# Hymba-style decoder step: a store and a state piece issued behind the next up loads on SyncE's queue

## Chip, core and metric

The kernel runs on one core of a Trainium2 chip. The metric is the device time of one execution in microseconds, lower is better. TensorE does the matmuls, VectorE (DVE), ScalarE (ACT) and GpSimd (POOL) the elementwise work, and SyncE (SP) issues most DMAs. All DMAs of the core share 16 DMA engines.

## What is computed

One step of a decoder layer on 1032 tokens (1024 prompt, 8 samples) of width 1024: a mixer (an mLSTM head group and an HGRN2 head group), then a mixture of 16 gated-MLP experts, of which each token takes two, each part with a residual and a layer norm. The change touches the second part only:

```python
def _hmoe(x, w_rg, b_rg, w_re, b_re, w1, w3, w2):
    ...
    eid = g[:, None] * EXPERTS_PER_GROUP + top_i
    gate = jnp.einsum('nk,nke->ne', wts, jax.nn.one_hot(eid, N_EXPERTS, dtype=F32))
    a = jnp.einsum('nd,edf->nef', xt, w1)
    u = jnp.einsum('nd,edf->nef', xt, w3)
    hdn = jax.nn.silu(a) * u * gate[..., None].astype(x.dtype)
    return jnp.einsum('nef,efd->nd', hdn, w2).reshape(B, T, D)
```

Each expert has a gate and an up matrix (1024x256) and a down matrix (256x1024), 1 MB each in f32. The step also returns new states of the 8 samples (`out_C_s`, `out_S_s`).

## The kernel before

The first 770 us are projections and the chunked mixer. Then come the router and the expert stage, from 805 us to 1086 us of the span, in 20 expert steps (`STEPS`), numbered 0 to 19 here. In a step 128 rows (tokens sorted by expert) are worked on, 32 for each of four streams (`STREAMS`). A stream walks through its experts in order, so a weight matrix is loaded only when the stream's next step has another expert; a load has a condition register (`cond=new`) and moves nothing otherwise. In a run of the expert stage 15 experts are loaded so, beside the four that were there at the start. Each stream has one buffer for each of the gate, up and down matrices, so a matrix can be loaded only once the products with the old one are over.

TensorE's order in step n: gate products of n (L1387), transposition of the hidden rows of n-1 (L1373), transposition of the x rows of n+1 (L1347), down products of n-1 (L1362), up products of n (L1398). Undisturbed a step takes about 11.8 us.

SyncE runs a queue in written order. In step n it waits for `gate_done` of n and issues the gate loads of n+1 (L1251); it waits for `down_done` of n-1 and issues the down loads of n (L1257); then `store_y(n - 1)` (L1284) waits until VectorE has added the down products of n-1 to the scaled residual (`y_read`) and stores 128 rows (512 KB) to `y_slots` in DRAM; in odd steps 3 to 17 `store_states` (`out_dma`, L474) stores one eighth of the samples' states, 512 KB; then SyncE waits for `up_done` of n and issues the up loads of n+1 (L1254). Ahead of the gate loads, and again ahead of the down loads, it reads the expert numbers and flags from SBUF (L1263, TENSOR_LOAD). In even steps up to 14 a load of `v_piece` (512 KB, L1272) follows the gate loads, and the 1 MB of layer-norm parameters for the end (L1311) are issued once, between steps 11 and 12.

The rows of x (512 KB for each step) are gathered by GpSimd on a queue of its own, q0. `ysb` has four buffers: ScalarE fills that of step n for n+4 once its store has landed. GpSimd gathers the stored rows only after the last store.

Of the kernel before, what the change touches and what calls it, by code (L numbers as in the profile page):

```python
# [31 lines left out]
H = 4  # L32
# [81 lines left out]
def _program(nc, t, ctx):  # L114
# [358 lines left out]
    def out_dma(eng, dst, src):  # L473
        eng.dma_start(dst, src).then_inc(s.outputs, 16)  # L474
        outs[0] += 1
# [41 lines left out]
    def x_rows(c):  # L517
        return P if c < NCH else NS
# [7 lines left out]
    def sync_rest(sp):  # L526
# [29 lines left out]
        for n, c in enumerate(ROW_ORDER):  # L556
# [26 lines left out]
            sp.dma_start(x1_dram[c * P:c * P + r], xrow_of(c)[0:r]).then_inc(s.x1_written, 16)  # L583
        sp.wait_ge(s.x1_written, 16 * NTT)
        sync_moe(sp)

    def samples_product(pe, bank, groups):
# [643 lines left out]
    def is_first(pair, i=0):  # L1231

        return isinstance(pair, int) and pair == 0 and i == 0
# [11 lines left out]
    def sync_moe(sp):  # L1245
        wg = t["w_gate"].rearrange("e (p k) f -> e p k f", k=KD)
        wu = t["w_up"].rearrange("e (p k) f -> e p k f", k=KD)
        wd = t["w_down"].rearrange("e (p k) n -> e p k n", k=2)

        def load_gate(q, expert, new):  # L1250
            sp.dma_start(w_gate[q], wg[bass.ds(expert, 1)].rearrange("e p k f -> p (e k) f"), cond=new).then_inc(s.w_gate_in, 16)  # L1251

        def load_up(q, expert, new):
            sp.dma_start(w_up[q], wu[bass.ds(expert, 1)].rearrange("e p k f -> p (e k) f"), cond=new).then_inc(s.w_up_in, 16)  # L1254

        def load_down(q, expert, new):
            sp.dma_start(w_down[q], wd[bass.ds(expert, 1)].rearrange("e p k n -> p (e k) n"), cond=new).then_inc(s.w_down_in, 16)  # L1257

        def experts_of(n):

            def words(w, top):
                row = step_loads[0:1, bass.ds((n * 2 + w) * STREAMS, STREAMS)]
                return nc.values_load_multi_w_load_instructions(row, engines=[mybir.EngineType.SP], min_val=0, max_val=top,  # L1263
                                                                skip_runtime_bounds_check_because="experts are minima with NE - 1, flags come from a comparison")[1]

            experts, flags = words(0, NE - 1), words(1, 1)
            return [(q, experts[q], flags[q]) for q in range(STREAMS)]

        def load_v(piece):
            if piece >= 1:  # L1270
                sp.wait_ge(s.state_added, 2 * piece)
            sp.dma_start(v_piece, v_dram[piece:piece + 1].rearrange("a (b v) -> a b v", b=NS).partition_broadcast(P).rearrange("p a b v -> p (a b) v")).then_inc(s.v_piece_in, 16)  # L1272

        sp.wait_ge(s.experts_known, 1)
        early_outs.append(outs[0])

        def store_states(piece):
            kind, at = piece // H, 8 * piece % HB
            sp.wait_ge(s.state_added, 2 * piece + 2)
            out_dma(sp, (t["out_C_s"], t["out_S_s"])[kind].rearrange("p h b v -> p (h b) v")[:, at:at + 8], (C0, S0)[kind][:, at:at + 8])  # L1280

        def store_y(n):
            sp.wait_ge(s.y_read, 2 * n + 2)
            sp.dma_start(y_slots[n * P:(n + 1) * P], ysb[n % YBUFS]).then_inc(y_out[n % YBUFS], 16)  # L1284

        def step(pair, i, last):
            n = pair * 2 + i
            if not (last and i == 1):
                coming = experts_of(n + 1)
                sp.wait_ge(s.gate_done, pair * 2 + (i + 1))  # L1290
                for q, expert, new in coming:
                    load_gate(q, expert, new)
                if i == 0 and pair < 2 * H:
                    load_v(pair)
            if not is_first(pair, i):
                present = experts_of(n)
                sp.wait_ge(s.down_done, n)
                for q, expert, new in present:
                    load_down(q, expert, new)
                store_y(n - 1)  # L1300
                if i == 1 and 1 <= pair <= 2 * H:
                    store_states(pair - 1)
            if not (last and i == 1):
                sp.wait_ge(s.up_done, pair * 2 + (i + 1))
                for q, expert, new in coming:
                    load_up(q, expert, new)

        def between(pair):

            if pair == 6:  # L1310
                sp.dma_start(ln2_gb, t["ln2"].partition_broadcast(P)).then_inc(s.ln2_in, 16)  # L1311

        for pair in range(STEPS // 2):
            between(pair)
            for i in range(2):
                step(pair, i, pair == STEPS // 2 - 1)
        store_y(STEPS - 1)
        early_outs.append(outs[0])
        for n, c in enumerate(ROW_ORDER):
            r = x_rows(c)  # L1320
            if n < Y_SHIFTED:
                sp.wait_ge(s.y_ready, n + 1)
            else:
                sp.wait_ge(s.y_last, NCH + n - Y_SHIFTED)
            out_dma(sp, t["out_y"][c * P:c * P + r], pair_of[c][0:r, 0])
        sp.wait_ge(s.outputs, 16 * outs[0])
# [823 lines left out]
```

## Time and profile before

| | us |
|---|---|
| median of three runs | 1131.74 |
| lowest and highest run | 1127.57, 1140.96 |
| profiled execution, its own time | 1135.78 |
| its span from first to last instruction | 1133.9 |
| TensorE busy | 1052.6 |
| SyncE's DMA queue q1 | 125.96 MB |

The trace is of one execution, and its span is 1.9 us under that execution's time. TensorE is busy for 93% of the span, with a mean granted clock of 0.972 of full speed. Where it stands still in the expert stage, the chain of waits names what it stood for.

### The profile page before, as it was taken

What the parts mean: (1) busy time and instruction counts of PE and PEld (TensorE: products, weight loads), DVE (VectorE), ACT (ScalarE), POOL (GpSimd) and SP (SyncE); (2) the same over time, 40 slices, a digit from 0 to 9 for tenths busy, and PEclk for the clock granted to TensorE, in tenths of its full rate; (3) what the DMA queues carried; (4) which work ended last, traced back from release to release, by engine and by line L of the source; (5) the groups of instructions that cost most, each with busy time, mean ns of one, the idle gap of its engine ahead of it and who ended that gap; (6) DMA issues with size and microseconds to landing.
All of it is one profiled execution on the core that took longest, in us unless ns stands there. A gap on an engine that the chain in (4) does not pass through costs nothing.

```text
span 1133.9 us, 17432 instructions
## 1 busy us (share of the span) xinstructions
PE 1052.6 (93%) x6876; PEld 621.2 (55%) x6876; DVE 543.7 (48%) x987; ACT 273.8 (24%) x557; POOL 211.2 (19%) x202
## 2 busy tenths in 40 slices
PE   7999999979999988899999999999889899899856
PEld 4666666645656545565665666655444554455322
DVE  1541033354564547668666765837334333332137
ACT  1552111121222223323332333311111111111113
POOL 0000000000110113245435534500100000000056
PEclk9999999989999989899999999999999999899978
DMA  9120202020000054201011001059599986957756
GB/s 380 62 75 1 75 1 74 1 78 0 2 0 1 1 182 174 89 20 38 1 38 38 20 19 38 19 204 373 210 380 344 350 298 190 368 205 234 249 207 259
DMA packets 30476, 150.10 MB, mean 132 GB/s; under 512 B 5603, under 2 KB 6051, under 8 KB 21323
## 3 DMA queue, kind: packets, MB, share of 16 engines
q1 hardware_dynamic: 24730, 125.96, 30.0%
q0 software_dynamic: 5248, 18.94, 4.7%
q10 hardware_dynamic: 432, 4.35, 1.0%
q8 instruction: 38, 0.62, 0.2%
q14 instruction: 28, 0.22, 0.1%
HBM read 317.31 MB, written 23.82 MB: 301 GB/s over the span
## 4 chain that ended last, share of the span: by engine, by line
PE 83%; DMA 8%; DVE 5%; issue 2%; SPq 1%; ACT 0%; POOL 0%; DVEq 0%; POOLq 0%; ACTq 0%
PE psum L1725 18%; PE psum L784 10%; PE psum L1776 10%; PE psum L797 8%; PE psum L1398 5%; PE psum L1362 5%; PE psum L825 4%; DMA x_cm<-in_w_up 4%; PE psum L1387 4%; PE psum L1410 2%; PE psum L1743 1%; DMA hg_q<-in_w_down 1%; PE psum L759 1%; PE psum L1347 1%; DMA weight_slots<-in_w_gate 1%
## 5 line engine op out<-in xcount | busy, mean ns | idle before, releaser
L1725 PE MATMUL psum<-x_cm,weight_slots 128*128 128x344 f32 x720 | 209.0, 453 | 0.0
L1725 PEld LDWEIGHTS psum<-x_cm,weight_slots 128*128 128x128 f32 x720 | 136.6, 190 | 71.9 <-issue 1.1
L1776 PE MATMUL psum<-weight_slots,x_cm 128*128 128x512 f32 x256 | 113.6, 597 | 0.0
L1362 PE MATMUL psum<-conv_qk,scratch 128*32 128x512 f32 x320 | 75.9, 618 | 7.9 <-DMA hg_q<-in_w_down 3.5
L1398 PE MATMUL psum<-conv_qk,scratch 128*32 128x256 f32 x640 | 74.4, 386 | 9.1 <-DMA x_cm<-in_w_up 9.1
L1387 PE MATMUL psum<-weight_slots,scratch 128*32 128x256 f32 x1280 | 75.6, 389 | 6.5 <-DMA weight_slots<-in_w_gate 4.2
L1776 PEld LDWEIGHTS psum<-weight_slots,x_cm 128*128 128x128 f32 x256 | 47.9, 192 | 54.2 <-issue 54.2
L1362 PE MATMUL psum<-hg_q,scratch 128*32 128x512 f32 x320 | 75.9, 619 | 0.0
L1398 PE MATMUL psum<-hg_decay,scratch 128*32 128x256 f32 x320 | 74.2, 386 | 0.0
L1398 PE MATMUL psum<-x_cm,scratch 128*32 128x256 f32 x320 | 74.2, 386 | 0.0
L825 PEld LDWEIGHTS psum<-scratch 128*128 128x128 f32 x448 | 58.7, 193 | 24.4 <-issue 22.7
L1479 POOL DMA_INDIRECT scratch<-x_rows,hg_k x20 | 19.0, 948 | 276.4 <-ACT scratch L1434 110.6
L1041 POOL TENSOR_TENSOR scratch<-scratch,hg_k 128x256 f32<-128x256 f32 x56 | 45.5, 812 | 104.5 <-ACT scratch L940 104.3
L1398 PEld LDWEIGHTS psum<-conv_qk,scratch 128*32 128x32 f32 x640 | 38.3, 111 | 46.3 <-DMA x_cm<-in_w_up 14.8
L1387 PEld LDWEIGHTS psum<-weight_slots,scratch 128*32 128x32 f32 x1280 | 43.8, 113 | 35.8 <-issue 6.1
L825 PE MATMUL psum<-scratch 128*128 128x128 f32 x448 | 59.8, 277 | 2.0 <-POOL scratch L1041 2.0
L2002 DVE TENSOR_SCALAR scratch<-scratch,small 128x1024 f32<-128x1024 f32 x8 | 6.5, 813 | 114.9 <-ACT scratch L1861 114.9
L1129 DVE COPY_PREDICATED scratch<-level_masks,psum 128x512 f32<-128x512 uint8 x64 | 46.9, 734 | 25.7 <-PE psum L827 22.5
L784 PE MATMUL psum<-weight_slots,x_cm 128*128 128x512 f32 x128 | 58.2, 597 | 0.0
L940 ACT ACTIVATE scratch<-scratch 128x512 f32<-128x512 f32 x56 | 35.3, 630 | 93.9 <-DVE scratch L1124 93.8
L1944 POOL TENSOR_TENSOR scratch<-scratch,constants 128x512 f32<-128x512 f32 x8 | 10.2, 1272 | 256.5 <-ACT scratch L1917 256.5
L784 PE MATMUL psum<-conv_qk,x_cm 128*128 128x512 f32 x128 | 57.8, 594 | 0.0
(390 smaller groups left out, 1678.8 us busy)
## 6 DMA issues: line engine op xcount, KB each, us to landing
weight_slots<-in_w_gate SPq DMA_DIRECT2D x80, 1024.0 KB
conv_qk<-in_w_up SPq DMA_DIRECT2D x40, 1024.0 KB
conv_qk<-in_w_down SPq DMA_DIRECT2D x40, 1024.0 KB
hg_q<-in_w_down SPq DMA_DIRECT2D x40, 1024.0 KB
hg_decay<-in_w_up SPq DMA_DIRECT2D x20, 1024.0 KB
x_cm<-in_w_up SPq DMA_DIRECT2D x20, 1024.0 KB
weight_slots<-in_w_in SPq DMA_DIRECT2D x6, 2048.0 KB, 8.2
y_slots<-scratch SPq DMA_DIRECT2D x10, 512.0 KB, 7.9
```

Of the source, the lines that this page charges most:

```text
L784: i = mm(PS[:, bank, :], xT[:, k, c * P:(c + 1) * P], w_slot(g)[:, k, :], start=(k == 0), stop=(k == KD - 1))
L797: i = mm(PS[:, 6 + n, :], lhs, w_out[:, e, n * 512:(n + 1) * 512], start=(e == 0), stop=(e == 7))
L825: i = mm(hp(2 + n % 2, h), xl[:, h], xl[:, h], start=True, stop=True)
L940: tell(A(xlev[n % 2], xlev[n % 2], ACT.Exp), s.level_exp)
L1041: tell(g.tensor_tensor(x, x, y, ALU.mult), s.level_scaled)
L1129: tell(v.copy_predicated(amat, msk[:, l:l + 1, :].to_broadcast([P, H, P]), by_h(PS[:, 2 + n % 2, :])), s.level_kept)
L1362: m = mm(PS[lane, 5 + half, :], hidT[:, k, lane], w_down[q][:, k, half * 512:(half + 1) * 512], start=(k == 0), stop=(k == 1))
L1387: m = mm(PS[lane, 2, 0:FF], xgT[i][:, k, lane], w_gate[q][:, k], start=(k == 0), stop=(k == KD - 1))
L1398: m = mm(PS[lane, 3, 0:FF], xgT[i][:, k, lane], w_up[q][:, k], start=(k == 0), stop=(k == KD - 1))
L1410: m = mm(PS[:, 2 * (n % 4) + half, :], ident, pair_of[c][:, k, half * 512:(half + 1) * 512], start=(k == 0), stop=(k == 1))
L1725: i = mm(PS[0:m, idx % 4, 0:PIECE], lhs_of(k), xT[:, k, n * PIECE:(n + 1) * PIECE], start=(k == 0), stop=(k == KD - 1))
L1776: i = mm(PS[:, bank, :], xT[:, k, c * P:(c + 1) * P], w_slot(g)[:, k, :], start=(k == 0), stop=(k == KD - 1))
```

## The change

The two stores move as a block from behind the down loads to behind the up loads. Nothing else differs: the same DMAs of the same size and the same waits. In step 19, which has no up loads, and after it the order is as before.

```diff
                 for q, expert, new in present:
                     load_down(q, expert, new)
-                store_y(n - 1)
-                if i == 1 and 1 <= pair <= 2 * H:
-                    store_states(pair - 1)
             if not (last and i == 1):
                 sp.wait_ge(s.up_done, pair * 2 + (i + 1))
                 for q, expert, new in coming:
                     load_up(q, expert, new)
+            if not is_first(pair, i):
+                store_y(n - 1)
+                if i == 1 and 1 <= pair <= 2 * H:
+                    store_states(pair - 1)
```

The helpers that it calls are these:

```python
def store_states(piece):
    kind, at = piece // H, 8 * piece % HB
    sp.wait_ge(s.state_added, 2 * piece + 2)
    out_dma(sp, (t["out_C_s"], t["out_S_s"])[kind].rearrange("p h b v -> p (h b) v")[:, at:at + 8], (C0, S0)[kind][:, at:at + 8])

def store_y(n):
    sp.wait_ge(s.y_read, 2 * n + 2)
    sp.dma_start(y_slots[n * P:(n + 1) * P], ysb[n % YBUFS]).then_inc(y_out[n % YBUFS], 16)
```

SyncE's queue at the seam of steps 11 and 12, before. The down loads write `conv_qk` and `hg_q`, the up loads `conv_qk`, `hg_decay` and `x_cm`, the gate loads `weight_slots`:

```order
L1257 DMA hg_q<-in_w_down 128x2048
L1284 DMA y_slots<-x_cm 128x1024
L474 DMA out_S_s<-weight_slots 128x1024
L1254 DMA conv_qk<-in_w_up 128x2048 x2
L1254 DMA hg_decay<-in_w_up 128x2048
L1254 DMA x_cm<-in_w_up 128x2048
L1311 DMA hg_k<-in_ln 128x2048
L1263 TENSOR_LOAD hg_k x2
L1251 ISA
L1251 DMA weight_slots<-in_w_gate 128x2048
```

The same place with the change (lines behind the diff count one higher):

```order
L1257 DMA hg_q<-in_w_down 128x2048
L1254 DMA conv_qk<-in_w_up 128x2048 x2
L1254 DMA hg_decay<-in_w_up 128x2048
L1254 DMA x_cm<-in_w_up 128x2048
L1284 DMA y_slots<-x_cm 128x1024
L474 DMA out_S_s<-weight_slots 128x1024
L1312 DMA hg_k<-in_ln 128x2048
L1263 TENSOR_LOAD hg_k x2
L1251 ISA
L1251 DMA weight_slots<-in_w_gate 128x2048
```

Both stores have moved past the four up loads and stand directly ahead of what follows in the next step. In an even step the block is the store of rows alone. The difference at such a place, the store of step 1's products in step 2:

```order
-L1284 DMA y_slots<-scratch 128x1024
-L1254 DMA conv_qk<-in_w_up 128x2048 x2
-L1254 DMA hg_decay<-in_w_up 128x2048
-L1254 DMA x_cm<-in_w_up 128x2048
-L1263 TENSOR_LOAD hg_k x2
```

The store of rows stood ahead of the up loads there; with the change it stands between them and the two TENSOR_LOADs.

## Rows read from the trace of the kernel before

**Rows 1.** The page, chain that ended last: share of the span by engine

```profile
PE 83%; DMA 8%; DVE 5%; issue 2%; SPq 1%; ACT 0%; POOL 0%; DVEq 0%; POOLq 0%; ACTq 0%
```

**Rows 2.** TensorE's waits from 805 to 1095 us: total, times, longest

```profile
PE psum L1398 <- DMA x_cm<-in_w_up: 9.1, 5, 3.4
PE psum L1387 <- DMA weight_slots<-in_w_gate: 4.2, 2, 3.7
PE psum L1362 <- DMA hg_q<-in_w_down: 3.5, 2, 2.5
PE psum L1362 <- issue: 2.7, 2, 2.1
```

**Rows 3.** Timeline of SyncE's queue in step 5: start, length, instruction

```profile
886.21 0.34 SPq L1284 DMA_DIRECT2D y_slots<-scratch  x1
886.60 1.31 SPq L474 DMA_DIRECT2D out_C_s<-x_cm  x1
888.24 0.54 SPq L1254 DMA_DIRECT2D conv_qk<-in_w_up  x2
...
891.92 1.14 SPq L1251 DMA_DIRECT2D weight_slots<-in_w_gate  x4
```

**Rows 4.** Timeline of TensorE: matmuls behind a wait, in brackets the idle time

```profile
845.97 0.41 PE L1398 MATMUL psum<-conv_qk,scratch 128*32 128x256 f32 x2 [3.40 <-DMA x_cm<-in_w_up]
...
871.98 0.41 PE L1398 MATMUL psum<-conv_qk,scratch 128*32 128x256 f32 x2 [1.50 <-DMA x_cm<-in_w_up]
...
881.09 0.62 PE L1362 MATMUL psum<-conv_qk,scratch 128*32 128x512 f32 x2 [0.69 <-issue]
...
897.68 0.41 PE L1398 MATMUL psum<-conv_qk,scratch 128*32 128x256 f32 x2 [1.14 <-DMA x_cm<-in_w_up]
...
908.17 0.62 PE L1362 MATMUL psum<-conv_qk,scratch 128*32 128x512 f32 x2 [2.06 <-issue]
...
982.13 1.50 PE L1387 MATMUL psum<-weight_slots,scratch 128*32 128x256 f32 x11 [3.67 <-DMA weight_slots<-in_w_gate]
...
1069.87 0.41 PE L1398 MATMUL psum<-conv_qk,scratch 128*32 128x256 f32 x2 [0.87 <-DMA x_cm<-in_w_up]
```

**Rows 5.** Busy time by stretch; last: PEclk, DMA share, GB/s

```profile
853.50:854.40 0.90, 0.90 (x13) 0.78 (x15) 0.42 (x1) 0.04 (x1) 0.00 (x0) 1.00 0.17 64
...
861.90:863.50 1.60, 1.57 (x32) 0.97 (x36) 1.53 (x4) 0.00 (x0) 0.00 (x0) 1.00 1.02 415
...
966.00:967.00 1.00, 1.00 (x27) 0.60 (x20) 0.20 (x1) 0.00 (x0) 0.00 (x0) 1.00 1.02 414
...
968.00:973.50 5.50, 5.50 (x70) 2.91 (x66) 2.42 (x4) 2.02 (x3) 0.00 (x0) 1.00 1.01 332
...
1022.00:1023.00 1.00, 1.00 (x24) 0.63 (x20) 0.96 (x3) 0.00 (x0) 0.00 (x0) 1.00 1.01 397
...
1062.00:1068.00 6.00, 5.48 (x78) 2.34 (x70) 0.42 (x1) 1.67 (x2) 0.00 (x0) 1.00 0.56 186
```

**Rows 6.** The chain that ended last, in order of time: start, length

```profile
854.40 3.57 PE psum L1362 x32
...
938.45 9.20 DMA hg_q<-in_w_down
...
968.14 1.20 SPq L1263
969.37 0.87 SPq L1263
...
982.13 6.30 PE psum L1387 x64
...
995.59 6.91 DMA hg_q<-in_w_down
...
1041.64 3.50 PE psum L1398 x64
...
1055.60 5.39 PE psum L1398 x64
```

## The prediction

> **What bounds the kernel now.** I read the chain that ended last first: TensorE holds 83% of it, DMA 8% [rows 1]. So the time is mostly matmuls that the change leaves alone, and only what TensorE stands still for can move. In the expert stage, the only stage with the edited queue, its waits for weights sum to four groups [rows 2]: up loads 9.1 us in five places, gate loads 4.2 us in two, down loads 3.5 us in two, and 2.7 us in two places that the view gives to "issue" and that stand at down products too. The first group is what the change can shorten, since the up loads are what the stores get out of the way of. The other three are where a gain can be lost again.
>
> Where the five up waits lie is read from TensorE's timeline [rows 4]: step 2 (3.40 us, at 845.97), step 4 (1.50), step 6 (1.14) and step 19 (0.87). These are 6.91 of the 9.1, so the fifth, before the up products that begin at 1055.60 in step 18 [rows 6], is 2.2 us. If all five went and nothing else moved, the gain would be 9.1 us, 0.8% of 1131.74. That is the ceiling without the clock.
>
> **The price of a store.** At 1022 the queue carries nothing but the stores issued in step 15, at a DMA share of 1.01 and 397 GB/s [rows 5]. 524 KB (128 x 1024 x 4 bytes) at that rate are 1.3 us for each, 2.6 us for both in odd steps 3 to 17. This is what leaves the way of the up loads, wherever the queue is full when they are issued. The same bytes then stand in the way of what comes behind: the next gate and down loads. The sum of bytes does not change, so while the DMA engines are full nothing is gained for the loads after the up loads.
>
> **Steps 2 to 7, gain and return.** Step 2: one store (1.3 us) goes from ahead of two new up matrices, so the up products begin at 844.7 instead of 845.97. The down products of step 2 follow, at 854.40 [rows 6]. Their loads have the same bytes ahead of them as before. The engines fall to a share of 0.17 from 853.50 to 854.40 [rows 5], so those loads were in by about 853.5, and 0.9 us at most of the 1.3 is kept. Step 4: the store and a state piece, 2.6 us, go; the wait of 1.50 goes whole. But the next down products, at 881.09, already waited 0.69 us [rows 4], and their loads again have unchanged bytes ahead: the 1.50 come back there. Step 6: the 1.14 go, and the down products at 908.17, which waited 2.06 us, take them back.
>
> There is a loss that works against the 0.9 us. Before, the stores are issued when VectorE has read the down products, some 2 us ahead of the up loads: 886.21 and 886.60 against 888.24 in step 5 [rows 3]. If the queue is short then, their data moves in time that is otherwise empty; behind the up loads it moves in time that is wanted. At 861.90 to 863.50, where step 3's stores could fill such a hole, the share is 1.02 [rows 5]; part of this is a gather of x rows that would fill the hole anyway. I bound this loss by nothing and by one full block, 2.6 us, and take 0.9, because the gathers and the stores share the holes. Steps 2 to 7 then give **0 us**, with ends of -0.9 and +2.6.
>
> **Step 10.** A down load of one matrix takes 9.20 us from its issue at 938.45, with both stores issued right behind it; two matrices in step 13, with both stores behind them as well, take 6.91 [rows 6]. If the stores slowed the first one, its wait of 2.5 us [rows 2] could go, but the second case says they need not. I take **0**, ends -2.5 and 0.
>
> **Step 13, a loss.** The largest gate wait, 3.67 us at 982.13 [rows 4], is for loads that came in behind a full queue: step 11's two stores, one up matrix, the 1 MB of layer-norm parameters, two gate matrices. From 968.00 to 973.50 the share is 1.01 [rows 5]. Before, most of the stores' data had moved by 968, ahead of the up matrix: the share from 966.00 to 967.00 is 1.02 at 414 GB/s [rows 5], and at the same rate to 968 that is 0.83 MB of 1.05. With the change SyncE issues nothing between the down loads and the end of the up products, so these 2 us stand empty and the 2.6 us of stores go between the up matrix and the gate loads that TensorE waits for. The loss is 2.0 to 2.6 us; I take **+2.3**. The next down wait follows a load issued after down products that are themselves later, so it does not pay this back.
>
> **Steps 18 and 19, a gain that stays.** In step 18 the up wait of 2.2 us goes: the store and states issued in step 17, 2.6 us, stood ahead. Behind it no gate or down load is waited for. In step 19 the store of step 18 leaves the way of the last up loads, worth up to the 0.87 us; but at 1062 to 1068 the engines have a share of only 0.56 [rows 5], so bytes alone do not explain that wait. I take half of it, 0.4. Together **-2.6**, ends -3.1 and -1.0 (a gate load of step 19 that becomes late takes back 1.2 of the 2.2).
>
> **SyncE's own time.** Behind the up loads it has about 2.1 us of TENSOR_LOADs (1.20 and 0.87 [rows 6]) before it can issue the next step's gate loads; behind step 5 these go out at 891.92, 3.7 us after the first up load [rows 3], about when the 3.5 us of gate products end. So there is no slack: the stores' 0.39 us (886.21 to 886.60), and 0.4 to 1.3 us more for the states, delay the gate loads by 0.8 to 1.7 us behind an odd step, by 0.4 behind an even one. I cost that at nothing: of the gate loads issued behind odd steps TensorE waits only for those of step 13, and they meet a queue that is full; without that cover it would be up to 1.7 us there. Behind SyncE's moved waits stands nothing that is not ready: VectorE has read the down products long before the up products end. ScalarE's buffers have four steps of slack, and the last stores keep their place.
>
> **The clock.** Two stalls are followed by half the granted clock: gate products of 6.30 us in step 13 and up products of 5.39 us in step 18, against 3.50 in an undisturbed one [rows 6]. Half the clock is 1.2 GHz, full 2.4. In step 18 the wait goes, and with it perhaps the 1.9 us of the slow products; a longer stall elsewhere could cost as much. I take 0, ends -1.9 and +1.9.
>
> **Sum.** 0 + 0 + 2.3 - 2.6 + 0 = -0.3 us: 1135.5 for an execution like the profiled one (1135.78), and **1131.4** from the median of 1131.74. The profiled execution is 4 us slower than the median, inside the spread of the three runs. Runs of this kernel differ by 13 us, so under 1%, 11 us, a measurement can hardly tell it from no change.
>
> **Rivals.** *The gain is kept* (0.15). The down waits behind steps 4 and 6 do not grow, since the gathers leave room: all five up waits go, -9.1, and -1.9 if step 18 keeps its clock: 1120.7 to 1122.6. For it: the up waits are the largest group. Against: the waits at 881.09 and 908.17, on unchanged bytes. *Slower, by holes in the queue* (0.17). Each block of stores that used to fill the time between the end of the down and of the up products now meets a load that is waited for: 2.6 us at the down products of step 4, 2.6 at those of step 6, 2.3 at the gate products of step 13, less the 2.6 of the end: about +5, 1136.7. It decides once queue and gathers are both empty at the end of the down products in steps 3 and 5. *The change does nothing* (inside the forecast): where the queue is short, stores finish before the up loads start.
>
> *Late completion* (0.08). In step 10 a load with stores issued behind it took 9.20 us [rows 6], and no row tells a store's completion from its data. If a load's completion had to wait for the stores ahead, each block would cost the gate loads behind it some further time; priced at one store's 1.3 us and paid at step 13, it gives -0.3 + 1.3, so 1132.7. The Trainium skill, DMA: Bandwidth & Descriptors, section "Queues, rings and completion order", says that a semaphore increment lands only after every earlier write of that DMA engine, which speaks against stores directly ahead of gate loads; but it speaks equally for clearing the up loads of them.
>
> **Chances and range.** The forecast (within some 3 us of 1131.4) 0.60, gain kept 0.15, holes 0.17, late completion 0.08. The ends of the unknown costs add up to -6.4 and +6.1 at worst; with the runs' own scatter the range is 1126 to 1138, which leaves out most of the first rival. Faster by over 1% needs all of the gain and the clock too: 0.04. Slower by over 1% needs twice the holes: 0.03. Within 1%: 0.93.
>
> **What would show it.** In the new profile: up waits in steps 2, 4, 6 and 18 together under 4 us; down waits in steps 4 to 7 larger by what the up waits lost; the gate wait of step 13 near 6 us; gate loads issued up to 1.7 us later behind odd steps; total weight waits within 3 us of before. I am wrong if the gate wait of step 13 does not grow, or if the down waits do not take over.

## The result and the profile after

The changed kernel takes 1140.41 us (median of 20 runs), the kernel before 1136.49 over 20 runs of its own. The ratio is 1.0041, 95% interval 1.0022 to 1.0060: 0.4% **slower**, 4.7 us by the ratio and 3.9 us between the two medians. (The three runs shown at first had a median of 1131.74; 20 runs put it 4.8 us higher, so the scatter of that starting point is as large as the effect.)

The profiled execution after took 1146.12 us, the highest of its 20 runs (the lowest is 1134.69), so its waits are read for their places and only roughly for their sizes. Lines from the old L1307 on stand one higher than before. The page's first line, and the chain that ended last by engine, to compare with [rows 1]:

```profile
span 1144.3 us, 17432 instructions
...
PE 81%; DMA 7%; DVE 6%; issue 3%; SPq 2%; ACT 0%; POOL 0%; another core or an unknown queue 0%; DVEq 0%; POOLq 0%; ACTq 0%
```

SyncE's own instructions have grown from 1% to 2% of the chain. TensorE's waits in the expert stage after, for [rows 2]:

```profile
PE psum L1388 <- DMA weight_slots<-in_w_gate: 9.8, 3, 6.6
PE psum L1363 <- issue: 5.7, 3, 2.1
PE psum L1388 <- issue: 5.2, 3, 3.5
PE psum L1399 <- DMA x_cm<-in_w_up: 5.1, 3, 2.8
PE psum L1363 <- DMA hg_q<-in_w_down: 3.0, 2, 2.2
```

The waits ahead of up products fell from 9.1 to 5.1 us, and from five places to three. Those ahead of gate products, for DMA, rose from 4.2 to 9.8 us. Where they lie is seen in the timeline of TensorE after, for [rows 4]:

```profile
822.54 2.08 PE L1388 MATMUL psum<-weight_slots,scratch 128*32 128x256 f32 x23 [3.49 <-issue]
...
847.56 0.64 PE L1399 MATMUL psum<-conv_qk,scratch 128*32 128x256 f32 x2 [2.81 <-DMA x_cm<-in_w_up]
...
875.35 0.41 PE L1399 MATMUL psum<-conv_qk,scratch 128*32 128x256 f32 x2 [1.35 <-DMA x_cm<-in_w_up]
...
885.32 0.62 PE L1363 MATMUL psum<-conv_qk,scratch 128*32 128x512 f32 x2 [1.54 <-issue]
...
901.69 0.41 PE L1399 MATMUL psum<-conv_qk,scratch 128*32 128x256 f32 x2 [0.94 <-DMA x_cm<-in_w_up]
...
912.28 1.07 PE L1363 MATMUL psum<-conv_qk,scratch 128*32 128x512 f32 x2 [2.14 <-issue]
...
935.05 2.40 PE L1388 MATMUL psum<-weight_slots,scratch 128*32 128x256 f32 x28 [2.33 <-DMA weight_slots<-in_w_gate]
...
991.51 1.93 PE L1388 MATMUL psum<-weight_slots,scratch 128*32 128x256 f32 x16 [6.56 <-DMA weight_slots<-in_w_gate]
...
1071.30 1.93 PE L1388 MATMUL psum<-weight_slots,scratch 128*32 128x256 f32 x32 [1.04 <-issue]
```

The up waits of steps 18 and 19 are gone; those of steps 2, 4 and 6 are still there. New is a gate wait of 2.33 us in step 9 (935.05). That of step 13 grew from 3.67 to 6.56. The first row, in step 1, comes ahead of any moved store: 3.49 us there against 1.7 before is scatter between executions.

The wait of step 9 explains itself in the chain that ended last, after: the two moved stores, two reads of expert words, the gate loads.

```profile
921.88 0.34 SPq L1284
...
922.27 0.42 SPq L474
...
922.74 3.76 SPq L1263
...
926.53 0.95 SPq L1263
...
928.83 6.18 DMA weight_slots<-in_w_gate
935.05 5.35 PE psum L1388 x64
```

The two TENSOR_LOADs take 4.7 us, where [rows 6], at the seam of steps 11 and 12, had 1.20 and 0.87. The timelines of TensorE and SyncE after give the lateness: the gate products of step 8 run from 920.74 for 3.64 us, to 924.4. The gate loads of step 9 may go out once these are over, and go out at 927.75, 3.4 us later (before, 0.3 us).

```profile
920.74 3.64 PE L1388 MATMUL psum<-weight_slots,scratch 128*32 128x256 f32 x64
...
927.75 1.43 SPq L1251 DMA_DIRECT2D weight_slots<-in_w_gate  x4
```

At the seam of steps 11 and 12 the chain shows the same: stores, layer-norm load, reads of 1.55 and 2.73 us.

```profile
974.11 0.34 SPq L1284
...
974.50 0.42 SPq L474
...
974.96 0.95 SPq L1312
...
975.96 1.55 SPq L1263
977.53 2.73 SPq L1263
...
982.14 9.32 DMA weight_slots<-in_w_gate
991.51 6.54 PE psum L1388 x64
```

From here on the **lateness** of a step is the start of its first gate load, less the end of its gate products, less the usual 0.29 us. Summed over steps 1 to 18 it is 18.4 us, against 4.1 us before. The down loads, measured in the same way against the down products that they wait for, are late by 8.1 us in sum, against 0.2 before.

### The profile page after: what moved, and what is told of

It reads as the page before. It is cut to its first block, busy times and chain, and to the rows that moved or that the text cites. A ratio compares the mean times of both kernels' runs of the same rounds, so it can differ in the third digit from the quotient of the medians.

```text
span 1144.3 us, 17432 instructions
## 1 busy us (share of the span) xinstructions
PE 1056.9 (92%) x6876; PEld 622.1 (54%) x6876; DVE 543.9 (48%) x987; ACT 273.8 (24%) x557; POOL 211.3 (18%) x202
## 4 chain that ended last, share of the span: by engine, by line
PE 81%; DMA 7%; DVE 6%; issue 3%; SPq 2%; ACT 0%; POOL 0%; another core or an unknown queue 0%; DVEq 0%; POOLq 0%; ACTq 0%
PE psum L1726 18%; PE psum L784 10%; PE psum L1777 10%; PE psum L797 8%; PE psum L1363 5%; PE psum L1399 5%; PE psum L1388 5%; PE psum L825 4%; DMA x_cm<-in_w_up 2%; PE psum L1744 1%; DMA hg_q<-in_w_down 1%; DMA weight_slots<-in_w_gate 1%; PE psum L759 1%; PE psum L1348 1%; DVE hg_decay L1670 1%
## 5 line engine op out<-in xcount | busy, mean ns | idle before, releaser
L1388 PE MATMUL psum<-weight_slots,scratch 128*32 128x256 f32 x1280 | 79.2, 403 | 15.1 <-DMA weight_slots<-in_w_gate 9.8
```

The costliest lines, as they stand in the source:

```text
L1388: m = mm(PS[lane, 2, 0:FF], xgT[i][:, k, lane], w_gate[q][:, k], start=(k == 0), stop=(k == KD - 1))
```

## Experiments

Theory A: SyncE is late, since it reads the expert words directly behind the stores. Theory B: the bytes of the moved stores stand ahead of the loads that TensorE waits for. Each experiment was timed beside the kernel before, and its ratio is to that: 1136.01 us for numbers 1 to 4, 1135.75 for 5 to 8, 1134.17 for 9 to 11. Waits and lateness are those of one profiled execution each, and differ between executions by a microsecond and more in a place.

**1. Words read ahead of the moved stores.** To the change:

```diff
-                coming = experts_of(n + 1)
+                coming = held.pop() if held else experts_of(n + 1)
...
                     load_up(q, expert, new)
+            if n + 2 < STEPS:
+                held.append(experts_of(n + 2))
             if not is_first(pair, i):
                 store_y(n - 1)
```

> The change, but the two reads of expert words for the next gate loads stand ahead of the moved stores instead of behind them. In the profile of the change these reads take up to 3.8 us behind the stores (0.87 us undisturbed), and gate loads go out up to 3.6 us late. Theory A (the reads behind the stores make SyncE late): the reads are short again, gate loads at most 1.5 us late, and the time comes back to within 0.2% of the kernel before. Theory B (the stores' bytes stand ahead of gate loads): the bytes' order is that of the change, so it stays about 0.4% slower.

Measured: 1131.51 us, ratio to before 0.9957 (0.9929 to 0.9985), 0.4% **faster**. The order of the DMAs is that of the change; only a read of 32 bytes stands elsewhere, and it turns 0.4% slower into 0.4% faster. Lateness sums to 1.5 us. TensorE's waits:

```profile
PE psum L1392 <- DMA weight_slots<-in_w_gate: 8.7, 3, 5.8
PE psum L1367 <- issue: 6.0, 4, 2.3
PE psum L1403 <- DMA x_cm<-in_w_up: 3.6, 3, 2.5
```

Theory B as the cause of the loss falls. (Behind the reads the stores themselves are issued some 1.9 us later than in the change. Number 7 tests SyncE's time without moving a store.) Something of theory B stays: the gate wait of step 13 is 5.8 us though its loads are on time within 1.1 us, against 3.67 before.

**2. Both stores behind the next gate loads.** To the kernel before; `stores(n - 1)` issues the rows of n-2 and the states that belong to step n-1:

```diff
                     load_gate(q, expert, new)
+                if n >= 2:
+                    stores(n - 1)
...
-                store_y(n - 1)
-                if i == 1 and 1 <= pair <= 2 * H:
-                    store_states(pair - 1)
```

> Both stores issued behind the next step's gate loads. Up and gate loads are both clear of the stores, which now stand ahead of the next down loads. Theory A: no lateness of gate loads, so 0 to 0.3% faster than before. Theory B: the stores' bytes only meet the down loads, whose waits grow by what the up waits lose; within 0.3% of before, with down waits of 8 us or more in place of 6.

Measured: 1139.09 us, 1.0017 (0.9992 to 1.0043), no difference shown. The waits moved to the down products, as both theories allow:

```profile
PE psum L1369 <- issue: 12.4, 5, 2.9
...
PE psum L1394 <- DMA weight_slots<-in_w_gate: 4.1, 2, 3.1
```

The reads ahead of the down loads now stand directly behind the stores, and the longest of all reads is 3.85 us here. The down loads are 17.4 us late in sum, up to 3.6 us in a step, while the gate loads are on time within 1.0 us. So SyncE's lateness has only gone to another load: clearing the gate loads alone is not enough, and the expected gain did not come.

**3. An extra read that was not there.** One more `experts_of(n + 1)` behind the up loads of the kernel before, its result unused.

> The kernel before, stores in their old place, with one more pair of reads of expert words (unused) behind the up loads, some 1.8 us of SyncE's time before the gate loads. No byte moves in another order. Theory A: gate loads 1.5 to 2 us late in all steps, gate waits grow, 0.2 to 0.5% slower. Theory B: within 0.1% of before.

Measured: 1138.26 us, 1.0016 (0.9988 to 1.0044). The trace has 74 reads, as before: the unused one is not in the program. So this says nothing on either theory. It is a repeat of the kernel before and shows what a timing is worth: 0.16% off, inside its interval.

**4. Stores issued by ScalarE**, in their old place in time:

```diff
-                store_y(n - 1)
                 if i == 1 and 1 <= pair <= 2 * H:
-                    store_states(pair - 1)
+                    outs[0] += 1
...
+            if n >= 1 and n < STEPS:
+                act.wait_ge(s.y_read, 2 * n)
+                act.dma_start(y_slots[(n - 1) * P:n * P], ysb[(n - 1) % YBUFS]).then_inc(y_out[(n - 1) % YBUFS], 16)
...
```

> The kernel before, but ScalarE issues the stores of rows and states on its own DMA queue as soon as VectorE has read the down products; SyncE only issues loads. Theory A: SyncE never late for gate loads, and the reads stay short; 0.1 to 0.4% faster than before. Theory B: the bytes move when they did before; within 0.2% of before.

(The states follow in the same way.) Measured: 1141.34 us, 1.0026 (0.9999 to 1.0053): no gain, rather a loss. Lateness is small (2.3 us in sum; before 4.1), so theory A's forecast of a gain failed. TensorE's waits ahead of down products are 15.7 us here, for 6.2 before, though the down loads go out on time:

```profile
PE psum L1361 <- issue: 12.1, 6, 4.0
PE psum L1397 <- DMA x_cm<-in_w_up: 4.4, 3, 1.9
...
PE psum L1361 <- DMA hg_q<-in_w_down: 3.6, 2, 2.1
```

So late issue is not the only thing that can cost time here. Why the down products wait most was not pursued.

**5 and 6. One store moved alone.** Number 5 moves the rows and leaves the states, number 6 the reverse. Number 5, written as an edit to the change:

```diff
                     load_down(q, expert, new)
+                if i == 1 and 1 <= pair <= 2 * H:
+                    store_states(pair - 1)
...
                 store_y(n - 1)
-                if i == 1 and 1 <= pair <= 2 * H:
-                    store_states(pair - 1)
```

> Only the store of rows is moved behind the up loads; the states stay between down and up loads. Theory A (reads of expert words directly behind stores take long and make the gate loads late): one store in front of the reads instead of two, so lateness of 0 to 1.7 us in every step but not 3 us; half of the loss or less, 0 to 0.2% slower than before. Theory B (bytes): 2.6 us fewer between up and gate loads per odd step; also in between. The lateness in odd steps tells them apart: A wants it under 2 us.

> Only the states are moved behind the up loads, in the eight odd steps that have them. Theory A: the reads behind the states are long (over 2 us) in odd steps and at 0.87 us in even ones; gate loads 1.5 to 3 us late in odd steps; 0.1 to 0.4% slower than before. Theory B: the up waits shrink as with the change and the gate wait of step 13 grows by 1.3 us; within 0.2%.

Measured: rows only 1136.37 us, 1.0000 (0.9980 to 1.0020); states only 1132.99 us, 0.9979 (0.9959 to 0.9999). No cost of either alone is shown; both together cost 0.4%. Lateness is 10.9 and 8.1 us in sum and at most 2.2 and 1.8 us in a step, under the 3.1 and 3.6 us of the change. That fits a limit. In the place where the change waits 2.33 us, the gate products of step 9, TensorE starts without a wait in both: their gate loads are 1.3 and 1.4 us late there, for 3.1 in the change. Where between these the limit lies is not shown. The forecast for number 6 (0.1 to 0.4% slower) was wrong.

**7. SyncE's time alone.** The kernel before, the words for the gate loads read twice:

```diff
-                coming = experts_of(n + 1)
+                coming, again = experts_of(n + 1), experts_of(n + 1)
+                coming = [c if q % 2 == 0 else a for q, (c, a) in enumerate(zip(coming, again))]
```

> The kernel before with its stores in their place, but the expert words for the gate loads are read twice, by four TENSOR_LOADs instead of two, half of the loads using the second reading (in the earlier try with an extra read the compiler left the unused read out). It adds 1.8 us or more of SyncE's time ahead of each gate load. Theory A: gate loads 1 to 2.5 us late in all steps, 0.2 to 0.5% slower. Theory B: within 0.1% of before.

Measured: 1141.19 us, 1.0058 (1.0032 to 1.0085), 0.6% slower, with every byte in the order of before. Lateness is 28.6 us in sum, and gate waits lead the list:

```profile
PE psum L1388 <- DMA weight_slots<-in_w_gate: 11.7, 3, 5.0
PE psum L1363 <- issue: 9.0, 4, 4.2
PE psum L1399 <- DMA x_cm<-in_w_up: 5.3, 2, 3.1
```

SyncE's time alone makes a loss of this size, with no store moved. (The down loads are late too, by 7.5 us in sum, as in the change.) It shortens the up waits as well (5.3 for 9.1 us), by moving the wait to an earlier product. The places are not those of the change: the gate waits are in steps 4 (3.63 us), 6 (3.07) and 13 (4.97), and there is none in step 9, where the loads are 1.5 us late.

**8. Words read ahead of the moved stores, and kept for the down loads.** To number 1:

```diff
+                kept.insert(0, coming)
...
-                present = experts_of(n)
+                present = kept.pop()
```

> The change with the words read ahead of the moved stores (as in the first experiment) and kept for the down loads of the next step, so one pair of reads in a step instead of two. Theory A: SyncE is nowhere late; as fast as the first experiment or up to 0.2% faster, that is 0.4 to 0.6% faster than before. Theory B: no gain over the change, 0.4% slower than before (already against the first experiment).

Measured: 1127.75 us, 0.9934 (0.9909 to 0.9959), 0.7% faster than before. Lateness 2.0 us in sum. Waits for up loads are down to 1.9 us:

```profile
PE psum L1393 <- DMA weight_slots<-in_w_gate: 7.1, 2, 5.7
PE psum L1368 <- issue: 6.0, 4, 2.0
...
PE psum L1404 <- DMA x_cm<-in_w_up: 1.9, 2, 1.6
```

**9 and 10. Kept words with either order, reads in their old place.** Number 9 is the kernel before, number 10 the change, each with the edit of number 8 to it: one pair of reads in a step, ahead of the gate loads; in number 10 it stands behind the stores.

> The kernel before with its stores in their place, but the words read for the gate loads are kept for the down loads, so one pair of reads in a step. Theory A (SyncE's time): the lateness of gate loads, 4.1 us in sum before, stays small, since the reads ahead of the gate loads remain; the gain over before is 0 to 0.2%, and what the experiment with moved stores and kept words has beyond it (0.66% in all) is the worth of the stores' new place. Theory B' (all of that gain comes from fewer reads): this one is 0.5% or more faster than before too.

> The change with the words kept for the down loads: one pair of reads in a step, and it still stands behind the moved stores. Theory A: what counts is the read behind the stores, so gate loads are late as with the change (12 us or more in sum), 0.2 to 0.5% slower than before. Theory B' (the number of reads counts, not their place): as fast as the version with words read ahead of the stores, 0.5% or more faster than before.

Measured: number 9 1129.89 us, 0.9966 (0.9939 to 0.9993); number 10 1134.75 us, 1.0005 (0.9983 to 1.0026). Number 10 has as few reads as number 8 and the same DMA order, yet is 0.7% slower; its lateness is 18.2 us, as with the change. Its SyncE timeline at the seam of steps 11 and 12, and that of number 8:

```profile
966.19 0.34 SPq L1284 DMA_DIRECT2D y_slots<-x_cm  x1
966.58 0.43 SPq L474 DMA_DIRECT2D out_S_s<-weight_slots  x1
967.05 0.90 SPq L1315 DMA_DIRECT2D hg_k<-in_ln  x1
972.39 1.70 SPq L1251 DMA_DIRECT2D weight_slots<-in_w_gate  x4
```

```profile
962.59 0.07 SPq L1254 DMA_DIRECT2D x_cm<-in_w_up  x1
964.53 0.34 SPq L1284 DMA_DIRECT2D y_slots<-x_cm  x1
964.92 0.43 SPq L474 DMA_DIRECT2D out_S_s<-weight_slots  x1
965.69 0.68 SPq L1317 DMA_DIRECT2D hg_k<-in_ln  x1
966.68 2.47 SPq L1251 DMA_DIRECT2D weight_slots<-in_w_gate  x4
```

In number 8 the gap of 1.9 us between the up loads (962.59) and the store (964.53) is the pair of reads, and the gate loads follow the layer-norm load at once. In number 10 the same pair sits in the gap from 967.95 to 972.39, 4.4 us. So it is the place of the read that counts. The number of reads seems to count too, some 0.3% in either order (1 to 0.9966, and 1.0041 to 1.0005, where the intervals just touch), more than theory A gave number 9. It would take back number 10's forecast loss of 0.2 to 0.5% against before. With no read ahead of them, number 10's down loads go out 0.06 us behind the down products as a rule, and are 1.6 us late in sum beyond that, for 8.1 in the change.

**11. Layer-norm parameters four steps later.** To number 8:

```diff
-            if pair == 6:
+            if pair == 8:
                 sp.dma_start(ln2_gb, t["ln2"].partition_broadcast(P)).then_inc(s.ln2_in, 16)
```

> Words read ahead of the moved stores and kept, and the 1 MB load of layer-norm parameters moved from between steps 11 and 12 to between steps 15 and 16. That load stands ahead of the gate loads of step 13, whose wait is 5.7 us there. If those waits are bytes in the queue, 1 MB at 400 GB/s is 2.6 us: the wait falls to about 3 us and the kernel is 0.2% faster than without the move, 0.8 to 0.9% faster than before. If the wait is issue and latency, it stays over 5 us and the time does not move.

Measured: 1125.14 us, 0.9925 (0.9899 to 0.9951), the fastest version, though not told apart from number 8 (0.9934) and 0.75% faster than before, where 0.8 to 0.9% was forecast. The gate wait of step 13, number 8 and then number 11:

```profile
979.26 2.36 PE L1393 MATMUL psum<-weight_slots,scratch 128*32 128x256 f32 x20 [5.72 <-DMA weight_slots<-in_w_gate]
```

```profile
979.88 2.75 PE L1393 MATMUL psum<-weight_slots,scratch 128*32 128x256 f32 x26 [2.92 <-DMA weight_slots<-in_w_gate]
```

It fell by 2.8 us for 1 MB, where 2.6 was forecast: with SyncE on time this wait is bytes. Part of it comes back: the gate products of step 17, whose loads now stand behind the moved 1 MB, wait 1.70 us, and in number 8 not at all.

## Why the prediction was wrong

The forecast was no change: -0.3 us, to 1131.4, and at most 1138. Measured were 1140.41 us and a loss of 4.7. Of the 9.0 us between forecast and result 4.8 are the starting point, a median of three runs; from 1136.49 the forecast would have been 1136.2. The rest is the loss that the sum did not hold. Of the signs named, the gate wait of step 13 came (near 6 us forecast, 6.56 found); the up waits under 4 us (5.1), lateness of 1.7 us at most (3.6) and waits within 3 us of before (19.5 to 23.6 us in the four groups) did not.

- **SyncE's own time: the step that failed.** The text took 2.1 us for the reads from one place, where up loads stood between them and the stores, priced the lateness at 0.8 to 1.7 us by the issue of the stores alone, and cost it at nothing, with no end in the range. The trace of before already had reads of up to 3.1 us, 1.9 us behind a store. The reads behind the stores take up to 4.7 us a pair and the loads were up to 3.6 us late (steps 8 and 12). The cover was wrong too: "TensorE waits only for those of step 13". It looked at waits before, not at how much slack each unwaited load had. The gate loads for step 9 went out 3.1 us late and TensorE waited 2.33 us for them, so on time they would have been some 0.7 us early in that execution. The gate products that follow fall to half the clock (0.50 granted from 936 to 937 us) and take 5.35 us for 3.64: 4.0 us in this one place. Experiments 1, 7 and 10 show that SyncE's time accounts for the whole loss and more: the same DMA order with reads ahead of the stores is 0.8% faster than the change (0.9957 against 1.0041).
- **The price of a store**, 1.3 us, stood; experiment 11's 2.8 us for 1 MB agrees.
- **Steps 2 to 7, "0 us".** In sum this held: the waits ahead of gate, up and down products there are 9.9 us before and 9.7 with the change (11.3 in number 1, 9.5 in number 8). The way there was only partly the one told. The up waits of steps 4 and 6 were said to go whole and stayed at 1.35 and 0.94 us, while the gate wait of step 4 rose from 0.51 to 0.94 and the down wait of step 5 from 0.69 to 1.54. In numbers 1 and 8 these up waits are smaller (0.64 and 0.48; nothing and 0.38), the down waits 1.4 to 2.3, and the gate wait of step 4 is 1.80 and 1.41. So the wait moves between products, and the exchange with the gate products was not foreseen. Lateness does not explain it: in steps 1 to 4 the change has none.
- **Step 10, taken as 0.** The down wait of 2.5 us went to 0.74 with the change and to 0.3 to 0.5 in numbers 1 and 10. The reasoning from step 13's pair of loads was wrong; the lower end of the term, -2.5, is near what came.
- **Step 13, +2.3.** Number 1, nearly on time, has 5.79 us against 3.67: +2.1 by bytes. The change's 6.56 us holds some lateness as well. Numbers 5 and 6, with one store moved, have 4.59 and 4.78.
- **Steps 18 and 19, -2.6.** The up waits went, with the slow clock of step 18, as forecast; but late gate loads put 0.70 and 1.04 us in their place, which the text had named as able to take back 1.2.
- **The clock** was taken as neutral. It was not neutral: in the expert stage the change's execution has products at half clock in steps 1, 2, 7, 9, 13, 14 and 19, the one before in steps 7, 13, 18 and 19. Part of that, in step 1, is scatter.
- **The rivals.** "Holes in the queue" gave 1136.7 and the right sign, which would have been luck: number 1, with the stores later still, is faster, so holes are not the cause of the loss, though step 13 pays for them as forecast. "The gain is kept" is matched in size once the read is moved: 0.4 to 0.7% faster, where 0.8% was the ceiling. It does not come in the way that this rival told, since step 13 still pays and steps 2 to 7 give little. "Late completion" would hold for number 1 as well, whose stores stand directly ahead of the gate loads, and that one is faster than before.

What stays open: why reads behind stores take so long, how the 0.3% of the second read splits between waits, and what the 1.9 us by which numbers 1 and 8 also delay the stores are worth by themselves.

## What to carry to other kernels

When an instruction is moved past others on an issuing queue, look at what it then stands directly ahead of: a register read from SBUF that feeds the next loads belongs ahead of the stores, and is best done once. For each load that the move delays, take its slack (products that need it, less its landing), not only whether it was waited for before. The reordering itself was good for 0.3 to 0.4%; a 32-byte read in the wrong place cost twice that.

## Hardware behaviour that was not expected

SyncE's TENSOR_LOAD of four words takes 0.87 us where no store was issued shortly before, whether the DMA engines are idle or busy with loads. In number 8 all 36 reads take 862 to 889 ns; the one at 1006.96 has a DMA share of 0.00, the one at 928.21 a share of 1.00 at 419 GB/s. The view of that line in number 8, in the kernel before and in the change (min, median, max in ns):

```profile
L1263 SPq TENSOR_LOAD <-hg_k x36: 862/867/889, 820.3 to 1042.6; - x36
```

```profile
L1263 SPq TENSOR_LOAD <-hg_k x74: 862/867/3137, 820.6 to 1062.8; - x74
```

```profile
L1263 SPq TENSOR_LOAD <-hg_k x74: 862/870/3759, 820.2 to 1073.0; - x74
```

Counted in the traces, with 4.5 us from the end of a store's issue to the start of a read as the bound: in the kernel before 29 reads are that near and take 1.27 us on average, 12 of them over 1.2 us; the 45 others take at most 0.89. In the change 42 are near (mean 1.50, 21 over 1.2). So about half of the near reads stay short, and what tells them apart is not known. The bound is rough too: a read 5.9 us behind a store took 1.18 us in the change, one 6.9 us behind took 2.26 in number 2. With the stores issued by ScalarE (number 4), reads still reach 3.0 us. The Trainium skill, DMA: Bandwidth & Descriptors, section "Latency and other measured facts", gives a floor of about 600 ns for this instruction; the traces' floor is 0.86 us, and the measurement decides.
